# Decoder trunk on one core: a ring of 22 slots under the front's tensors, gates and branch outputs with tokens on partitions, the attention loop unrolled, and a new order of loads

## What is computed

```python
xn = rms_norm(h, norm1_g)
q, kv, nsa_g, pool_u, conv_h, conv_b, conv_c, merge_g = split(xn @ w_in)      # w_in: 1024 x 5656
y_nsa  = nsa_mixer(q, kv, nsa_g, ...) @ w_nsa_proj    # 8 heads of 64, 2 kv groups
y_pool = pool_mixer(pool_u, ...) @ w_pool_proj        # causal means over 2, 4, 8, 16 tokens
y_conv = short_conv_mixer(conv_h, conv_b, conv_c, ...) @ w_conv_proj
mg = sigmoid(merge_g).reshape(256, 3, 1024)
h = h + (mg[:,0]*y_nsa + mg[:,1]*y_pool + mg[:,2]*y_conv) @ w_o
# 32 experts, 2 chosen for a token within one of 4 groups:
out = sum over e of combine[:, e] * ((silu(x2 @ w1[e]) * (x2 @ w3[e])) @ w2[e])   # x2 = rms_norm(h, norm2_g)
h = h + out;  return rms_norm(h, final_norm_g)
```

## Time and profile before

| | us |
|---|---|
| median of 3 executions | 445.52 |
| the profiled execution, its own time | 445.05 |
| its span in the profile | 443.2 |
| PE busy (matmuls) | 387.3 (87% of the span) |
| DVE busy | 201.0 (45%) |
| ACT busy | 150.3 (34%) |
| POOL busy | 19.0 (4%) |
| one high part (ACT, line 413), mean | 1.85 |
| one low part (DVE, line 420), mean | 2.22 |
| one load of line 465, from issue to landing, shortest and median | 4.7 and 7.5 |
| moved by DMA | 140.28 MB, mean 316 GB/s |

### The profile page before, as it was taken

How to read it: one execution, slowest core, us unless ns; L and a number is a source line. 1 busy time by engine, 2 the same in 40 slices (tenths; PEclk the granted TensorE clock), 3 DMA queues, 4 the chain that set the end, 5 groups by cost and what they waited for, 6 DMA issues and landing times.

```text
span 443.2 us, 7398 instructions
## 1 busy us (share of the span) xinstructions
PE 387.3 (87%) x2876; PEld 271.2 (61%) x2876; DVE 201.0 (45%) x382; ACT 150.3 (34%) x244; POOL 19.0 (4%) x46
## 2 busy tenths in 40 slices
PE   2999999999999999999979797979888797968971
PEld 2999999888988999898755152524343342414320
DVE  0957395887878673974481123121222211202113
ACT  5842342664556553522312121313022212103014
POOL 1000001100000000000110043000000000000001
PEclk9999999999999999999999999999999999969998
DMA  8993956263346453689798999999999999999972
GB/s 304 413 418 142 377 220 260 96 237 108 132 143 249 176 191 114 227 318 381 288 408 344 422 419 418 418 420 419 421 417 422 420 419 419 421 419 421 420 302 95
DMA packets 21335, 140.28 MB, mean 316 GB/s; under 512 B 2624, under 2 KB 3008, under 8 KB 5312
## 3 DMA queue, kind: packets, MB, share of 16 engines
q1 hardware_dynamic: 20304, 138.34, 78.1%
q10 hardware_dynamic: 1008, 1.62, 1.0%
HBM read 138.90 MB, written 1.05 MB: 316 GB/s over the span
## 4 chain that ended last, share of the span: by engine, by line
PE 70%; SPq 10%; DMA 7%; DVE 6%; ACT 3%; issue 2%; POOL 0%; DVEq 0%; POOLq 0%; ACTq 0%
PE bank L1168 11%; PE bank L1169 10%; PE bank L1170 10%; SPq L495 9%; PE bank L1506 8%; DMA ring<-in_experts 6%; PE bank L1479 5%; PE bank L1541 5%; PE bank L1532 5%; PE bank L1283 2%; PE bank L1410 2%; PE bank L1411 2%; PE bank L1412 2%; ACT gab L754 1%; PE bank L1310 1%
## 5 line engine op out<-in xcount | busy, mean ns | idle before, releaser
L1168 PE MATMUL bank<-xhi,part 128*128 128x256 f32 x320 | 92.9, 290 | 0.0
L1169 PE MATMUL bank<-xlo,part 128*128 128x256 f32 x320 | 90.6, 283 | 0.0
L1170 PE MATMUL bank<-xhi,part 128*128 128x256 f32 x320 | 90.6, 283 | 0.0
L1506 PE MATMUL bank<-ring,kv 128*32 128x512 f32 x512 | 60.4, 601 | 9.5 <-DVE kv L1101 6.4
L420 DVE TENSOR_TENSOR part<-ring,part 128x2048 fp32r<-128x2048 f32 (+1 forms) x28 | 61.6, 2219 | 7.9 <-ACT part L413 7.8
L1168 PEld LDWEIGHTS bank<-xhi,part 128*128 128x128 f32 x320 | 61.3, 192 | 5.9 <-issue 5.8
L1169 PEld LDWEIGHTS bank<-xlo,part 128*128 128x128 f32 x320 | 61.3, 192 | 0.0
L1170 PEld LDWEIGHTS bank<-xhi,part 128*128 128x128 f32 x320 | 61.3, 192 | 0.0
L413 ACT CAST part<-ring 128x2048 fp32r<-128x2048 f32 (+1 forms) x28 | 51.5, 1849 | 19.6 <-DMA ring<-in_front 19.6
L1115 DVE TENSOR_TENSOR h<-h,bank 128x512 f32<-128x512 f32 x32 | 22.0, 688 | 70.9 <-PE bank L1541 70.9
L1541 PE MATMUL bank<-gab,vbd 128*128 128x512 f32 x64 | 31.7, 618 | 12.3 <-ACT gab L754 12.3
(11 more groups left out here) (237 smaller groups left out, 511.5 us busy)
## 6 DMA issues: line engine op xcount, KB each, us to landing
ring<-in_experts SPq DMA_DIRECT2D x92, 1024.0 KB, 18.0
ring<-in_front SPq DMA_DIRECT2D x30, 1024.0 KB, 7.1
ring<-in_projs SPq DMA_DIRECT2D x4, 512.0 KB, 3.7
ring<-in_front SPq DMA_DIRECT2D x2, 560.0 KB, 17.6
h<-in_x SPq DMA_DIRECT2D x2, 512.0 KB, 3.8
oT<-in_vecs ACTq DMA_DIRECT2D x2, 512.0 KB, 8.1
squares<-in_experts SPq DMA_DIRECT2D x1, 1024.0 KB, 7.0
merged<-in_experts SPq DMA_DIRECT2D x1, 1024.0 KB, 15.4
```

The source lines that it names most:

```text
L1168: mm(dst, whi, ahi, start=start, stop=False)
L1169: mm(dst, whi, alo, start=False, stop=False)
L1170: return mm(dst, wlo, ahi, start=False, stop=stop)
L1506: ins = mm(bank[0][CAP * e:CAP * (e + 1)], xgT[:, q, CAP * e:CAP * (e + 1)], expert(j, q, e), start=(q == 0), stop=(q == NQ1 - 1))
```

## The change

The edits, as far as the steps below speak of them:

- The ring gets 22 slots. xhi, xlo, merged, oT and mixed lie in slots of the ring instead of beside it. The spare pieces and POOL's copies of them are gone. The slots are no longer piece modulo 16 but a table `AT`, and a load of piece c waits for the piece that lay in its slot before (`earlier`).
- Chunks of the front alternate between two sets of four slots instead of three.
- The merge gates are six chunks of 512 columns of one branch each; tokens are stationary (128 of them), and the weights move, 512 wide. The same holds for the branch projections and the attention's projection. `merged` has tokens on partitions, and 16 transposes on PE (`merged_turned`) turn it for the output projection.
- The loop is written out four times. Scores read qT itself; the copy to qcur is gone. Units 0 and 1 of the scores stand together as before, and units 2 and 3 too now.
- The GELU and the split of the first projection stand ahead of the loop on DVE and ACT.
- SP's order of loads is written out by hand.
- The last gain vector lies in con, and a scratch area of the program's DMA is set to 256.

```diff
-SLOTS = 16
+SLOTS = 22
-SET_C, SET_B, SET_A = 4, 8, 12
+SLOT_CMP = 0
+SLOT_FREE = 4
+SLOT_PROJ, SLOT_PROJHI, SLOT_MIX = 7, 8, 9
+SET_A, SET_B = 10, 14
+SLOT_XLO, SLOT_MERGED, SLOT_O, SLOT_XHI = 18, 19, 20, 21
+AT = [*range(SLOTS), *range(13), *range(4), *range(13, SLOTS)]
+CHUNK_SET = {n: (SET_A, SET_B)[i % 2] for i, n in enumerate(SPLITS)}
+HELD = {s: [c for c in range(NC) if AT[c] == s] for s in range(SLOTS)}
+def turn(c):
+    return HELD[AT[c]].index(c)
+def earlier(c):
+    return HELD[AT[c]][turn(c) - 1] - (NC if turn(c) == 0 else 0)
...
@@ SP @@
+            sp.dma_start(ident, consts[:, K_ID:K_ID + P]).then_inc(ident_in, 16)
+            front_chunk(CH_Q, 0)
+            front_chunk(CH_Q, 1)
+            sp.dma_start(con[:, P:], consts[:, P:]).then_inc(con_in, 16)
+            front_chunk(CH_KV, 0)
+            front_chunk(CH_KV, 1)
+            front_chunk(CH_CK, 0)
+            front_chunk(CH_CK, 1)
+            front_chunk(CH_VG, 0)
+            front_chunk(CH_VG, 1)
...
+            projections(0)
+            projections(1)
+            early(SLOT_FREE, SLOT_FREE + 1)
+            front_chunk(CH_BC, 0)
+            front_chunk(CH_BC, 1)
+            early(SLOT_FREE + 1, SLOT_PROJ)
...
+            sp.wait_ge(y_full, NT * N_LOOP)
+            early(SLOT_PROJ, SET_A)
+            front_chunk(CH_NSA, 0)
+            front_chunk(CH_NSA, 1)
+            for i in range(2):
+                front_chunk(CH_WO + i, 0)
+                front_chunk(CH_WO + i, 1)
+            sp.wait_ge(wo_used, 1)
+            early(SET_A, SET_A + 2)
+            sp.wait_ge(tr_full, 2 * NT)
+            early(SLOT_MERGED, SLOT_O)
+            sp.wait_ge(wo_used, 2)
+            early(SET_A + 2, SET_B)
+            sp.wait_ge(wo_used, 3)
+            early(SET_B, SET_B + 2)
+            sp.wait_ge(wo_full, 4)
+            early(SET_B + 2, SLOT_MERGED)
+            sp.wait_ge(lgT_full, 1)
+            early(SLOT_XHI, SLOTS)
+            sp.wait_ge(xn2_done, NT)
+            early(SLOT_O, SLOT_XHI)
+            for c in range(SLOTS, NC):
+                sp.wait_ge(expert_used, earlier(c) + 1)
+                sp.dma_start(ring[:, AT[c]], experts[c // NQ, c % NQ]).then_inc(expert_in[AT[c]], 16)
...
@@ DVE, ahead of the loop, which begins with scores(0), scores(1), weigh(0) @@
             nc.vector.tensor_tensor(hidu[:], hidu[:], hidg[:], ALU.mult).then_inc(gelu_in, 1)
+            def projection_low(i):
+                dve.wait_ge(projhi_done, i + 1)
+                nc.vector.tensor_tensor(projlo[:, i % 2].bitcast(F32R), proj(i), projhi[:, i % 2], ALU.subtract).then_inc(proj_split, 1)
             dve.wait_ge(tanh_done, 1)
...
+            projection_low(0)
...
@@ PE @@
+            def gate(n, half, t):
+                split(CH_MG + n, half)
...
+                for k in range(4):
+                    kk = 4 * half + k
+                    mm(bank[t][:], XH[:, kk, cols], whi[:, k], start=(kk == 0), stop=False)
+                    mm(bank[t][:], XH[:, kk, cols], wlo[:, k], start=False, stop=False)
+                    ins = mm(bank[t][:], XL[:, kk, cols], whi[:, k], start=False, stop=(kk == KT - 1))
...
+            for i in range(N_LOOP):
+                s_unit(4 * i)
+                s_unit(4 * i + 1)
+                gate(i, 0, 0)
+                gate(i, 0, 1)
+                t_unit(4 * i)
+                s_unit(4 * i + 2)
+                s_unit(4 * i + 3)
+                gate(i, 1, 0)
+                t_unit(4 * i + 1)
+                gate(i, 1, 1)
+                pv_units(i, 0)
+                t_unit(4 * i + 2)
+                mixed_part(i, 0)
+                t_unit(4 * i + 3)
+                mixed_part(i, 1)
+                pv_units(i, 1)
...
+            nsa(0, 0)
+            nsa(0, 1)
+            nsa(1, 0)
+            merged_turned(0)
+            nsa(1, 1)
+            pe.wait_ge(g_done, NT * N_G)
+            for j in range(4):
+                split(CH_WO + j // 2, j % 2)
+                pe.wait_ge(mlo_done, (2, 4)[j // 2])
+                for n in range(4):
+                    for k in (2 * j, 2 * j + 1):
+                        ins = output(n, k)
...
+                if j == 0:
+                    merged_turned(1)
...
-    nc = bacc.Bacc("TRN2", target_bir_lowering=False, num_devices=1)
+    nc = bacc.Bacc("TRN2", target_bir_lowering=False, num_devices=1, dynamic_dma_scratch_size=256)
```

More of the change, by code:

```diff
@@ new lines, in _, with front_chunk, projections @@
+                            CH_NSA: ((y_full, 2 * N_LOOP + NT), (y_full, 2 * N_G))}
+            for i in range(N_G):
+                last_product[CH_MG + i] = ((g_used, i + 1), (g_full, NT * (i + 1)))
+            def front_chunk(n, half):
+                if before(n):
+                    sp.wait_ge(*last_product[before(n)[-1]][half])
+                c = floats(n)
+                sp.dma_start(raw(n, half)[:, 0:c], front[n, half, :, 0:c]).then_inc(chunk_in[slot(n, half)], 16)
+            def projections(i):
+                if i >= 2:
+                    sp.wait_ge(y_full, NT * (i - 1))
+                sp.dma_start(proj(i), projs[i]).then_inc(proj_in[i % 2], 16)
@@ L440, in early_experts, with early @@
+            def early(first, end):
                 for c in range(first, end):
                     sp.dma_start(ring[:, c], experts[c // NQ, c % NQ]).then_inc(expert_in[c], 16)
-            def early_spare(n, free):
-                sp.wait_ge(*free)
-                b, q = divmod(first_spare + n, NQ)
-                w = SLOT // len(spare[n])
-                for i, piece in enumerate(spare[n]):
-                    sp.dma_start(piece, experts[b, q, :, i * w:(i + 1) * w]).then_inc(spare_in, 16)
@@ new lines, in _ @@
+            front_chunk(CH_MG + 2, 1)
+            projections(2)
+            front_chunk(CH_MG + 3, 0)
+            front_chunk(CH_MG + 3, 1)
+            projections(3)
+            for i in range(4, N_G):
+                front_chunk(CH_MG + i, 0)
+                front_chunk(CH_MG + i, 1)
+            sp.wait_ge(y_full, NT * N_LOOP)
[5 more added lines that the diff above has]
+                front_chunk(CH_WO + i, 1)
@@ new lines, in take_o @@
+            def take_o(i):
+                dve.wait_ge(pv_full, 2 * i + 2)
+                nc.vector.tensor_copy(oT[:, i], bank[7][:, 0:T]).then_inc(o_read, 1)
+            for i in range(N_LOOP):
+                scores(4 * i)
+                scores(4 * i + 1)
+                weigh(4 * i)
+                weigh(4 * i + 1)
+                if i > 0:
+                    take_o(i - 1)
+                    for t in range(NT):
+                        merge(i - 1, t)
+                have_low(dve, CH_MG + i + 1, 0)
+                scores(4 * i + 2)
+                scores(4 * i + 3)
+                weigh(4 * i + 2)
+                weigh(4 * i + 3)
+                have_low(dve, CH_MG + i + 1, 1)
+                if i + 1 < N_LOOP:
+                    projection_low(i + 1)
@@ L940, in _ @@
+            take_o(N_LOOP - 1)
             dve.wait_ge(kc_full, 1)
@@ L946, in _ @@
             ins.then_inc(kc_done, 1)
-            dve.wait_ge(merge_done, N_MG + 1)
-            dve.wait_ge(yp_full, N_MG)
-            step(nc.vector.memset(pc, 0.0))
-            have_low(dve, CH_M0B, 1)
-            have_low(dve, CH_NSA, 0)
+            for t in range(NT):
+                merge(N_LOOP - 1, t)
+            have_low(dve, CH_MG + 5, 0)
             dve.wait_ge(sc_full, 1)
@@ L1155, in turned @@
                         ins.then_inc(full, 1)
-            def keep_busy(n):
-                for _ in range(n):
-                    mm(bank[7][:, 0:2 * P], ident, con[:, K_TRI:K_TRI + 2 * P], start=True, stop=True)
             pe.wait_ge(diag_done, NT)
@@ L1186, in channels, with pair @@
                 return ins
-            def pair(dst, n, half, full, more=0):
-                split(n, half, more)
+            def pair(dst, n, half, full):
+                split(n, half)
                 for a in range(2):
@@ L1338, in _, with s_unit @@
-            pe.wait_ge(ga_done, N_MG + 1)
-            pair(bank[0], CH_M0A, 0, m0_full)
+            def s_unit(n):
+                i, u = n // 4, n % 4
+                g, b = u % 2, u // 2
+                rows = slice(g * HD, (g + 1) * HD)
+                if n >= 2:
+                    pe.wait_ge(s_max, n - 1)
+                for t in range(NT):
+                    ins = mm(bank[4 + u % 2][:, t * P:(t + 1) * P + t * P], qT[rows, i, t * P:(t + 1) * P],
+                             kT[rows, b, 0:(t + 1) * P], start=True, stop=True)
+                ins.then_inc(s_full, 1)
@@ L1378, in _ @@
             ins.then_inc(pcT_full, 1)
-            channels(bank[3][:, T:2 * T], w, P, range(0, 2))
+            gate(5, 0, 1)
             pe.wait_ge(pcT_done, 1)
@@ L1441, in _, with keep_busy @@
             ins.then_inc(lgT_full, 1)
+            def keep_busy(n):
+                for _ in range(n):
```

(1 more changed line is left out.)

619 lines of the change are left out of this document (266 added, 353 removed).

## The result

The changed kernel takes 448.04 us (median of 11 executions, 447.51 to 451.72), the kernel before took 444.96 beside it (11 executions). The ratio is 1.0104, 95% interval 1.0081 to 1.0127: some 4.6 us slower. Six of the eleven times lie at 447.51 to 448.04 us and five at 451.04 to 451.72. The profiled execution took 447.81 us with a span of 446.0, 2.8 us over the span of before.

A forecast was written before the change was run, and what follows sets the result against it. PE bounds the front, the DMA weight stream the experts. Front -1.7 us (-6.1 + 3.5 + 1.2 - 0.3) and ring +3.9 give +2.2 on 445.05: 447.2 profiled, 447.6 us median; range 442.5 to 451, forecast's own 445.0 to 449.5.

The forecast's parts named there:

- The ring: Expert weight loads: pieces 35 to 38 wait for slots of late pieces, DMA idle some 9 us; last landing +3.9 us.
- Rival 2: Expert weight loads: PE is done with pieces 22 to 25 when the queue comes to them; 438.8 us, chance 0.04.
- The loop: Attention loop on PE: wide matmuls and scores of units 2 and 3 together save 1.5 us an iteration, 6.1 in four.
- rival 4: Gates on PE: wide matmuls gain less than predicted; 451.9 us with no gain, 449.8 with half; chance 0.06.
- The wait at the loop's start: Before the loop's first transposes: GELU and low part of projection 0 raise PE's wait from 0.88 to 4.4 us, +3.5.
- Rival 1: Loop's start: no added wait, as DVE's and ACT's new work fits under PE's; 443.0 us, chance 0.22.
- The clock: Loop's start: PE's wait brings the lower clock, 0 to 1.7 us of work lost, taken as +1.2 us.
- Behind the loop: From loop to experts: wide matmuls -1.6, covered wait -1.0, 16 transposes +2.0, form changes +0.3; in all -0.3 us.
- rival 3: Start of the output projection: low part of an output chunk comes late, PE stands; 3 us lost, 450.6 us, chance 0.14.
- The sum: Whole kernel: front -1.7 us, behind the experts' start +3.9 us, together +2.2 us on the profiled execution's 445.05 us.

The follow-up runs named there:

- experiment 1: Changed kernel with another map of pieces to ring slots alone: 444.89 us, ratio 0.9988 against the kernel before.
- experiment 2: Changed kernel with a slot map fitted to the times at which PE is through with the pieces: 440.47 us, ratio 0.9905 against the kernel before.
- experiment 9: Changed kernel with the scores of units 2 and 3 apart again, as in the kernel before: 454.58 us, ratio 1.0224.
- experiment 5: Changed kernel with POOL's two splits of `mixed` waiting until DVE has ended the GELU: 447.02 us, ratio 1.0057 against the kernel before.
- experiment 4: Changed kernel with both halves of the first gate chunk loaded ahead of the early expert pieces: 447.16 us, ratio 1.0047 against the kernel before.
- experiment 6: Changed kernel with 14 matmuls without a use in PE's wait at the loop's start: 447.79 us, ratio 1.0058 against the kernel before.
- experiment 7: Changed kernel with 5 more matmuls without a use ahead of the experts: 448.52 us, ratio 1.0072 against the kernel before.
- experiment 11: experiment 10's kernel with POOL's splits of `mixed` waiting until DVE has weighed the first two units: 436.14 us, ratio 0.9801 against the kernel before.
- experiment 3: Changed kernel with the GELU and low part of projection 0 moved from the loop's head into iterations 0 and 1: 445.73 us, ratio 1.0021.
- experiment 10: Changed kernel with fitted slot map, GELU moved into the loop, first gate chunk loaded earlier, 5 more matmuls ahead of the experts: 432.93 us, ratio 0.9734.

## Why the prediction held, and where its sizes were off

The forecast was 447.6 us and slower; the median is 448.04. The steps were the right ones, but that the number is so close is partly luck. Two misses nearly cancel (see the sum), and the median lies in the lower of two groups of times by one execution of eleven; the five of the upper group, from 451.04 us on, all lie above the 451 us at which my range ends. Point by point:

- **The ring.** Right in cause and size; the hole came some 3 us sooner. I had the hole at 41 to 47 us behind the start; it is at 38 to 44. I had the last piece at 203.3 us behind the start and measured 202.05. The predicted loss of 3.9 us was a difference from a start with the lower clock; from the first read of a piece it is 4.0. Experiments 1 and 2 show that it is the map: another one turns it into a gain. Rival 2 (the refill isn't held up) is out. What the larger ring gives with a right map I had as 5 us sooner than before; counted from the first read it is 5.4 (experiment 2).
- **The loop.** Predicted 1.5 us an iteration, measured 1.60. The split was 0.86 for the scores together and 0.66 for the wide matmuls; experiment 9 gives 1.03 and a remainder of 0.57. In the gates a wide matmul comes every 0.228 us, so rival 4 is out. By the gap that "TensorE: Matmul & The Clock Gate" of the Trainium skill (Back-to-back issue gap) states for a matmul in isolation, 60 pairs save an estimated 0.15 us an iteration; the 0.57 left are nearer to the 0.66 of the rows.
- **The wait at the loop's start.** The step that was mis-sized: predicted 4.4 us, measured 6.96; the added idle time was 6.1 us and not 3.5. My chain from the copy of `hidg` to the first scores was right to 0.3 us where POOL is away: 81.22 us less 77.60, the copy in experiment 5, is 3.6 us, against 79.5 - 75.55 = 3.9. I left out two things: that the chain itself begins 1.87 us later, for the most part (1.7 us, experiment 4) because SP now issues expert pieces ahead of the halves of the first gate chunk (I had called the loads ahead of the loop covered), and that POOL's splits run beside DVE's small steps (1.5 us, experiment 5). The second could be read in the trace of before: POOL splits `mixed` from 75.70 to 79.63 there. Rival 1 is out.
- **The clock.** Predicted +1.2 us, measured 2: experiment 6 removes the dip and gains 1.8 us. The lower clock lasted 6.8 us (83.3 to 90.2), where I had 3.4 from the earlier trace rows; 2.7 of them passed in the wait and 4.1 on work.
- **Behind the loop.** Predicted -0.3 us. The lag against before is 100.47 - 94.16 = 6.3 us at the start of iteration 1; three iterations take 4.8 of it back, so 1.5 are left, and at the experts' start it is 0.2: the stages between gave 1.3 us. There the profile has PE busy 62.00 of 62 us, so no wait for a low part of the output chunks: rival 3 is out.
- **The sum.** Front predicted -1.7, measured +0.2: the misses of the wait (2.6) and the clock (0.8) outweighed those of the loop (0.3) and of what is behind it (1.0); these four make +0.4. Behind the start I had +3.9 and measured 202.05 - 199.4 = +2.65, since the first gathers of this execution took 2.94 us and I had reckoned with the 4.33 of before. So the span grew by 2.8 us, by my sum 2.2: 1.9 us too little for the front and 1.25 too much behind it, and that they meet is luck. The medians of the side-by-side runs are 3.1 us apart and the ratio says 4.6, for the changed kernel has its upper group of executions, 3.5 us longer at a lower granted clock, and its profiled one is not of these. That effect was in none of my terms, and where in an execution it arises stays open (experiment 7).

## What to carry to other kernels

When a ring of buffers grows, write down for every refill when its slot is given back and when the queue reaches it; the number of slots is worth nothing while one in-order queue stands behind a slot of a late piece. Work that is put at the head of a pipeline's first iteration costs its full chain there, whatever the average load of the engine says, and an idle TensorE pays a second time in clock. Two gains in different stages that both end in the same stream of loads add up: take the stage's own sum each time, and then run them together.

## What the runs showed of the hardware that I had not expected

- Where steps of DVE and POOL on on-chip tensors meet, the one that began first keeps its time and the other ends behind it. Steps of DVE of 120 columns took 0.59, 1.27 and 0.58 us beside POOL's split and 0.28, 0.22 and 0.28 without it (experiment 5). In experiment 11 DVE's step from 82.44 keeps near its 2.29 us (2.35), POOL's subtraction begun behind it takes 3.22 in place of 1.28 and ends at 85.94, and DVE's next, begun behind that one, takes 2.32 in place of 1.21. DVE's steps of 384 columns that read PSUM (`att<-con,bank`) kept their 0.6 us beside POOL (experiments 3 and 10).
- The clock fell in the experts' first microseconds in some profiles and not in others, with nothing changed ahead of them, and with PE busy 0.60 of 2 us ahead of them in the changed kernel's profile, where it stayed at 1.00, and 0.59 in that of experiment 1, where it fell. It cost 1.6 to 2.5 us on the first gathers (4.57 and 5.49 us against 2.94), and in experiment 6 the last piece is later behind the start by the same 1.6 us (203.64 against 202.05). In the profiles of the four kernels with five more matmuls without a use it did not fall; they delay the start by 0.6 us.
- With one dip of the clock removed, the profiled execution had another further on (experiment 6): a gain can be there in the trace and missing in the time. Which executions fall, and why, stays open.
